# The start of a two-layer kernel, with its first modulation split by chunks and its loads and modulation blocks in another order

## The reference

```
def ada_modulation(cond, w_mod, b_mod):
    m = jax.nn.silu(cond) @ w_mod + b_mod        # (1024) @ (1024, 6144)
    return jnp.split(m, N_MOD, axis=-1)          # shift, scale, gate, shift, scale, gate

# even layer
sh1, sc1, g1, sh2, sc2, g2 = ada_modulation(c, mod_w, mod_b)
csh1, csc1, cg1, csh2, csc2, cg2 = ada_modulation(c_ctx, mod_w, mod_b)
h = modulate(rms_norm(x, norm_mix), sh1, sc1) @ w_in      # w_in: (1024, 2048)
hc = modulate(rms_norm(xc, norm_mix), csh1, csc1) @ w_in
u, q, k, v = jnp.split(h, cuts, axis=-1)
# Fourier mixing of u; neighbourhood attention of q, k, v; x + g1 * (concat @ w_out); dense SwiGLU
```

## Time and profile before

| | us |
|---|---|
| median of 3 runs | 1858.24 (1858.16 to 1859.18) |
| the profiled execution | 1858.6 |
| its span, first to last instruction | 1856.8 |
| TensorE busy | 1787.1 |
| VectorE busy | 1242.8 |
| ScalarE busy | 1008.6 |
| GpSimd busy | 334.8 |

### The profile page before, as it was taken

One profiled execution on the slowest core, in us unless ns is written; L12 is line 12 of the kernel. 1 busy time (PEld: TensorE's weight loads), 2 busy tenths in 40 slices (PEclk: granted clock), 3 DMA queues, 4 the chain that ended last, 5 costly groups with the idle time before them and its releaser, 6 DMA issues.

```text
span 1856.8 us, 24922 instructions
## 1 busy us (share of the span) xinstructions
PE 1787.1 (96%) x8836; PEld 1392.3 (75%) x8836; DVE 1242.8 (67%) x1276; ACT 1008.6 (54%) x1098; POOL 334.8 (18%) x565
## 2 busy tenths in 40 slices
PE   5999999999999999899999999999999999999997
PEld 3667445888888886566788888888888888888886
DVE  3241515242424235745998989989899999998997
ACT  3222834222213121364677777777777777777774
POOL 6886821020201124101100001000000000000000
PEclk8999999999999999999999999999999999999999
DMA  9788612122223151502799999999999999999995
GB/s 371 297 348 302 269 70 91 68 104 100 91 80 125 46 210 57 170 2 91 272 370 383 355 373 364 369 380 355 371 373 361 377 360 366 379 360 373 364 370 205
DMA packets 72503, 481.57 MB, mean 259 GB/s; under 512 B 7984, under 2 KB 11184, under 8 KB 17584
## 3 DMA queue, kind: packets, MB, share of 16 engines
q1 hardware_dynamic: 69872, 472.92, 66.6%
q0 software_dynamic: 1424, 5.51, 0.7%
q10 hardware_dynamic: 1136, 2.21, 0.4%
HBM read 473.29 MB, written 7.32 MB: 259 GB/s over the span
## 4 chain that ended last, share of the span: by engine, by line
PE 90%; DVE 3%; DMA 3%; ACT 2%; issue 1%; SPq 0%; POOL 0%; ACTq 0%; DVEq 0%
PE bank L1090 32%; PE bank L1104 16%; PE bank L807 12%; PE bank L777 4%; PE bank L824 3%; PE bank L836 3%; PE bank L657 3%; PE bank L875 3%; PE bank L590 2%; DMA ring<-in_ev_mod 2%; PE bank L1073 1%; PE bank L745 1%; PE bank L637 1%; PE bank L728 1%; PE bank L1122 1%
## 5 line engine op out<-in xcount | busy, mean ns | idle before, releaser
L1855 DVE TENSOR_TENSOR rest<-ring,WR 128x2048 fp32r<-128x2048 f32 x336 | 765.6, 2306 | 80.6 <-ACT WR L1414 78.8
L1414 ACT ACTIVATE WR<-ring 128x2048 fp32r<-128x2048 f32 x336 | 634.7, 1919 | 68.9 <-DMA ring<-in_experts 66.4
L1090 PE MATMUL bank<-WR,xer 128*128 128x512 f32 x1792 | 579.0, 395 | 2.3 <-DVE B L2032 2.3
L1090 PEld LDWEIGHTS bank<-WR,xer 128*128 128x128 f32 x1792 | 336.4, 188 | 70.0 <-issue 2.5
L1090 PE MATMUL bank<-rest,xer 128*128 128x512 f32 x896 | 349.5, 390 | 0.0
L1104 PE MATMUL bank<-WR,heTr 128*128 128x512 f32 x896 | 279.9, 391 | 0.0
L807 PE MATMUL bank<-hTr,WR 128*128 128x512 f32 x672 | 207.4, 390 | 0.0
L1104 PEld LDWEIGHTS bank<-WR,heTr 128*128 128x128 f32 x896 | 168.2, 188 | 34.5
L1090 PEld LDWEIGHTS bank<-rest,xer 128*128 128x128 f32 x896 | 168.6, 188 | 32.4
L1104 PE MATMUL bank<-rest,heTr 128*128 128x512 f32 x448 | 174.4, 389 | 0.0
L1707 DVE TENSOR_TENSOR rest<-ring,WR 128x2048 fp32r<-128x2048 f32 (+2 forms) x38 | 80.3, 2115 | 123.9 <-ACT WR L1339 123.7
(11 more groups left out here) (354 smaller groups left out, 2143.7 us busy)
## 6 DMA issues: line engine op xcount, KB each, us to landing
ring<-in_experts SPq DMA_DIRECT2D x336, 1024.0 KB, 4.8
ring<-in_ev_mod SPq DMA_DIRECT2D x24, 1024.0 KB, 9.9
ring<-in_od_mod SPq DMA_DIRECT2D x24, 1024.0 KB, 8.3
ring<-in_ffn_up SPq DMA_DIRECT2D x22, 1024.0 KB, 6.9
ring<-in_ffn_down SPq DMA_DIRECT2D x12, 768.0 KB, 5.1
ring<-in_ev_in SPq DMA_DIRECT2D x8, 1024.0 KB, 6.6
ring<-in_ev_out SPq DMA_DIRECT2D x4, 1024.0 KB, 8.3
ring<-in_od_out SPq DMA_DIRECT2D x4, 1024.0 KB, 12.8
```

The source lines that it names most:

```text
L1090: mm = pe.matmul(bank[m % 2][:, :], xer[:, i, 4 * kh + k, :], w[j][:, 512 * k:512 * k + 512], start=(kh == 0 and k == 0 and x == 0), stop= ...
L1414: act.activation(part(0, h), ring[:, h % HALVES, :], ACT.Copy).then_inc(split_hi, 1)
L1855: dve.tensor_tensor(part(1, h), ring[:, h % HALVES, :], part(0, h).bitcast(F32), ALU.subtract).then_inc(split_lo, 1)
```

## The change

**The first modulation is by chunks.** The columns of the first four `ev_mod` slots are regrouped: slot b now holds 256 columns of the shift and 256 of the scale, those of chunks 2b and 2b + 1. Each of blocks 0 to 3 is a group of its own, with its row, its turn and its coefficients (`modulated_front`), and chunks 2b and 2b + 1 are modulated with it. Block 0 stands ahead of the projection, block 1 between the first turn and chunk 0, blocks 2 and 3 ahead of chunks 2 and 3. The 18 products that kept TensorE busy (`keep_busy`) go.

**The loads are reordered.** The first weights of the projection are loaded second, and SP no longer waits for the fourth block's landing before it loads them.

**The blocks are moved.** Blocks 4 to 17 stand in the projection (before: 4 to 16), 18 and 19 in the turns (before: 17), 20, 21 and 22 in the Fourier stage (before: 18), and 23 in step 0 of the attention (before: 19 to 23 in steps 0, 2, 4, 6 and 8). The third group's row and turn go from steps 9 and 10 to steps 1 and 2. The bias tables of heads 5 to 7 are loaded after all modulation blocks.

```
-EARLY = ([("mod", s) for s in range(4)]
-         + [("in", 0), ("mod", 4), ("mod", 5), ("mod", 6), ("in", 1), ("mod", 7), ("mod", 8), ("mod", 9),
...
-UNDER_TURN = {2: 17}
-UNDER_FOUR = {4: 18}
-UNDER_ATTN = {0: 19, 2: 20, 4: 21, 6: 22, 8: 23}
+EARLY = [("mod", 0), ("in", 0), ("mod", 1), ("mod", 2), ("mod", 3),
+         ("in", 1), ("mod", 4), ("mod", 5), ("mod", 6), ("mod", 7),
+         ("in", 2), ("mod", 8), ("mod", 9), ("mod", 10), ("mod", 11),
+         ("in", 3)] + [("mod", s) for s in range(12, 24)]
+EARLY_SLOT = [0, 1, 2, 0, 2, 0, 2, 2, 1, 2, 1, 2, 2, 0, 2, 0, 2, 2, 1, 2, 1, 2, 1, 2, 0, 1, 2, 0]
+UNDER_IN = {(0, 6): 4, (4, 4): 5, (5, 2): 6, (5, 7): 7, (7, 3): 8, (8, 7): 9, (9, 4): 10, (10, 1): 11, (11, 6): 12,
+            (13, 2): 13, (13, 7): 14, (14, 4): 15, (15, 1): 16, (15, 6): 17}
+UNDER_TURN = {3: 18, 7: 19}
+UNDER_FOUR = {2: 20, 4: 21, 7: 22}
+UNDER_ATTN = {0: 23}
-ROW_JOB = 9
+ROW_JOB = 11
-MOD_GROUPS = ((0, 4), (4, 12), (12, 24))
+FRONT = 4
+MOD_GROUPS = ((0, 1), (1, 2), (2, 3), (3, 4), (4, 12), (12, 24))
...
             for i, (what, n) in enumerate(EARLY):
-                if i == S_IN_E[0]:
-                    wait_slot(sp, S_MOD[3])
...
-                if i == S_MOD[22]:
-                    for h in range(5, NA_HEADS):
-                        load_bias(h)
...
+            for h in range(5, NA_HEADS):
+                load_bias(h)
...
             def w_in_even():
+                modulation(1)
                 for c in range(DC):
+                    if c in (2, 3):
+                        modulation(c)
...
+                    if c in (0, 2, 3):
+                        modulation_turn((1, 0, 2, 3)[c])
                 for j in range(4, 16):
                     n, t = divmod(j, 4)
-                    if j == 12:
-                        modulation_turn(1)
+                    if j == 13:
+                        modulation_turn(FRONT)
...
-            for s in range(4):
-                modulation(s)
-                if s == 1:
-                    norm_turn(0)
+            modulation(0)
+            norm_turn(0)
             modulation_turn(0)
-            keep_busy(18)
             w_in_even()
...
+            def modulated_front(b):
+
+                dve.wait_ge(mod_turned, b + 1)
+                o = mod_turn_bank(b)[0]
+                for at, m in ((0, M_SH1 + 2 * b), (4, M_SC1 + 2 * b)):
+                    ins = dve.tensor_tensor(mod[0][:, m:m + 2, :], o[:, at:at + 4].rearrange("p (b s) -> p b s", s=2),
+                                            vec[:, V_MODB + m:V_MODB + m + 2].unsqueeze(2).to_broadcast([P, 2, 2]), ALU.add)
+                step(ins)
+                k = coef[:, 0, 2 * b:2 * b + 2, :]
+                step(dve.tensor_scalar(k, mod[0][:, M_SC1 + 2 * b:M_SC1 + 2 * b + 2, :], 1.0, None, ALU.add))
+                dve.tensor_tensor(k, k, vec[:, V_NORM + 2 * b:V_NORM + 2 * b + 2].unsqueeze(2).to_broadcast([P, 2, 2]),
+                                  ALU.mult).then_inc(coef_front, 1)
+                dve.wait_ge(coef_front, b + 1)
...
             dve.wait_ge(ht_dve, 4)
-            for c in range(1, DC, 2):
+            for b in range(FRONT):
+                c = 2 * b + 1
+                if b:
+                    modulation_row(b)
+                modulated_front(b)
...
-                if c == 1:
+                if b == 0:
                     split_in(0)
...
+                if b == 1:
+                    split_in(1)
```

More of the change, by code:

```diff
@@ L52 @@
 UP_SLOTS, DOWN_SLOTS = FC // 2, 2 * len(FG)
-EARLY = ([("mod", s) for s in range(4)]
-         + [("in", 0), ("mod", 4), ("mod", 5), ("mod", 6), ("in", 1), ("mod", 7), ("mod", 8), ("mod", 9),
-            ("in", 2), ("mod", 10), ("mod", 11), ("mod", 12), ("mod", 13), ("in", 3)]
-         + [("mod", s) for s in range(14, 24)])
-EARLY_SLOT = [0, 1, 2, 0, 1, 2, 0, 2, 0, 2, 2, 1, 2, 1, 1, 0, 1, 0, 1, 2, 1, 2, 1, 2, 1, 2, 0, 1]
-UNDER_IN = {(0, 2): 4, (0, 3): 5, (0, 5): 6, (0, 7): 7, (5, 2): 8, (5, 7): 9, (7, 4): 10, (8, 7): 11, (9, 5): 12,
-            (10, 2): 13, (12, 0): 14, (13, 4): 15, (15, 0): 16}
-UNDER_TURN = {2: 17}
-UNDER_FOUR = {4: 18}
-UNDER_ATTN = {0: 19, 2: 20, 4: 21, 6: 22, 8: 23}
+EARLY = [("mod", 0), ("in", 0), ("mod", 1), ("mod", 2), ("mod", 3),
[8 more added lines that the diff above has]
+UNDER_ATTN = {0: 23}
 ROW_AT = max(UNDER_ATTN) + 1
 IN_BANK = (4, 5, 6, 2)
-ROW_JOB = 9
+ROW_JOB = 11
 S_MOD = [EARLY.index(("mod", s)) for s in range(24)]
 S_IN_E = [EARLY.index(("in", n)) for n in range(4)]
-MOD_GROUPS = ((0, 4), (4, 12), (12, 24))
+FRONT = 4
+MOD_GROUPS = ((0, 1), (1, 2), (2, 3), (3, 4), (4, 12), (12, 24))
 S_OUT_E, S_FFN = 28, 30
@@ L444, in mod_bank @@
         def mod_bank(g):
-            return bank[(0, 3, 7)[g]]
+            return bank[(0, 0, 0, 0, 3, 7)[g]]
         def mod_rows(g):
-            return (mrow[:, 0, :], mrow[:, 1, :], rows[:, 0:512])[g]
+            return rows[:, 0:512] if g == FRONT + 1 else mrow[:, g % 2, :]
         def mod_turn_bank(g):
-            return ((bank[1], 0), (bank[3], 0), (bank[6], 0))[g]
+            return (bank[(1, 1, 1, 1, 3, 6)[g]], 0)
         HALVES2 = (slice(0, HD), slice(HD, 2 * HD))
@@ L1218, in _ @@
             split_in(0)
-            act.wait_ge(coef_ready, 1)
             act.wait_ge(ht_act, 4)
-            for c in range(0, DC, 2):
+            for b in range(FRONT):
+                c = 2 * b
+                act.wait_ge(coef_front, b + 1)
                 for s in range(2):
@@ L1227, in _ @@
                 for cc in (c, c + 1):
-                    act.wait_ge(h0_act if cc == c else h0_dve, cc // 2 + 1)
+                    act.wait_ge(h0_act if cc == c else h0_dve, b + 1)
                     act.activation(h0r[cc], hT[:, cc, :], ACT.Copy).then_inc(h0_hi, 1)
+                if b == 0:
+                    split_in(1)
             act.dma_start(dft, a["dft"]).then_inc(dft_landed, 16)
-            for x in range(1, 4):
+            for x in range(2, 4):
                 split_in(x)
@@ L1603, in _ @@
             normed(0)
+            modulation_row(0)
             for c in range(1, DC, 2):
@@ L1642, in _ @@
                 if j == ROW_JOB:
-                    modulation_row(1)
+                    modulation_row(FRONT)
                 if t in (1, 2) and 1 <= n < 3:
@@ L2358, in strips @@
         return slots(w, [(at, 512) for at in range(0, w.shape[1], 512)])
-    arrays.update(ev_mod=strips(f["ev_mod_w"][0]), ev_in=strips(f["ev_w_in"][0]), od_mod=strips(f["od_mod_w"][0]),
+    w = f["ev_mod_w"][0]
+    first = [w[:, at + 256 * b:at + 256 * b + 256] for b in range(4) for at in (0, D)]
+    arrays.update(ev_mod=strips(np.concatenate(first + [w[:, 2 * D:]], 1)), ev_in=strips(f["ev_w_in"][0]), od_mod=strips(f["od_mod_w"][0]),
                   ev_out=strips(f["ev_w_out"][0]), od_out=strips(f["od_w_out"][0]),
```

18 lines of the change are left out of this document (8 added, 10 removed).

## The result

The changed kernel takes 1861.15 us (median of 20 runs, 1859.19 to 1865.55), the kernel before 1858.65 (20 runs, 1856.89 to 1860.84). The ratio is 1.0016, with a 95% interval of 1.001 to 1.0022: slower by 1.9 to 4.1 us, where 6.2 us faster was forecast. The profiled execution took 1860.71 us, with a span of 1858.8 us.

The account below looks back on a forecast made before the run. TensorE, busy 96% of the span, was taken as the bound, with all gain before 244 us. Fourier stage ending 1.5 us earlier plus attention 4.7 shorter gave 6.2 us off 1858.24: 1852.0 us, range 1849.5 to 1855 (wider: 1846.5 to 1857.5).

Parts of the forecast that it names:

- Part 1: Start of the kernel: first projection matmul at 29.8 us against 45.56, 15.7 us earlier.
- half clock of 2.2 us: Projection's start: TensorE at half clock for some 4 us, costing 2.2 us, bounds 0 and 5.6.
- Part 2: Projection: 124.8 us of work plus 2.2 for the clock and 0.8 of waits, ending at 157.6, 8.7 us earlier.
- the tightest pairs: Projection: ring-slot-sharing blocks 4 and 5, 7 and 8, 8 and 9, with 36 matmuls (8.2 us) between; waits put at 0.8 us.
- Part 3: Turns and Fourier stage: 25.4 us of work with five blocks, plus 1.5 of waits, ending at 184.5 against 186.0.
- 5.2 us a load: Turns and Fourier stage: pace of the modulation loads in a row, landing block 22 at 180.3 us.
- Part 4: Attention: four blocks leave its steps, making it 4.7 us shorter, bounds 1.0 and 7.7.
- Rival 3: Turns and Fourier stage: five loads pace TensorE at 7.1 us each, stage 8 us late, 1861.5 us; chance 0.09.
- bound of 187.2: Fourier stage: its latest end, in us, with loads at 5.8 us each.
- rival 1: Projection and Fourier stage: loads and clock cost nothing, gain 4.5 us more, 1847.5 us; chance 0.17.
- rival 2: Attention: VectorE's and ScalarE's chain replaces the blocks, 1 us won of 5.0, 1855.7 us; chance 0.13.
- rival 4: Front: chunk pipeline at VectorE's pace, three turns wait 2 us each, projection ends 6 us late, 1855 us; chance 0.08.

Follow-up runs that it names:

- e13_spread_both: Changed kernel with blocks 17 to 23 and tables of heads 5 to 7 placed as before, tables of heads 0 to 2 before block 13, GpSimd's stores later; 1848.41 us.
- e11_stores_later: Changed kernel with GpSimd's tables 8 to 12, and so their stores, made behind the bias tables of the attention; 1859.09 us.
- e4_half_loads: Changed kernel with loads of blocks 14 to 22 bringing half their bytes, TensorE multiplying as often; 1851.89 us.
- e12_after_both: Changed kernel with bias tables of heads 0 to 2 loaded before block 13 and GpSimd's stores of tables 8 to 12 behind the bias tables; 1856.77 us.

## Why the prediction was wrong

**Part 1 held.** The first matmul of the projection came at 29.74 us, forecast 29.8. The half clock of 2.2 us did not come; its lower bound, 0, was the value.

**Part 2 was 3 us short.** Its sum without waits and clock, 29.8 + 124.8 = 154.6, agrees with e13_spread_both: 155.52 us with one block less (2.1) and 2.8 us of waits for loads in it, so 154.8 on the same count. Waits were put at 0.8; they were 2.7 before block 14 and 1.7 elsewhere, and 1.5 more of half clock. The step that failed in this part: the tightest pairs were looked for by matmuls between blocks, and block 14's load was not followed through SP's list. It stood behind the 2 MB of block 13 and three tables, all issued in the 3 us before it, and took 14.23 us. The prediction did walk SP's queue past the tables before block 18, not past those before block 14. Its 7.51 us for a lone load was high, too: another load had 0.7 us left to land when that one's second half was issued at 65.94. Two 2 MB loads of the trace before with none ahead of them (second halves issued at 53.58 and 75.93) took 6.86 and 6.98 us, near the 6.8 that the prediction set aside.

**Part 3 is where the forecast broke, in the sentence "block 17 is issued when block 15 is done, at 145.2, and lands near 153".** It was issued at 147.5 and landed at 157.0. 2.3 us of that came with block 15, which ran late behind block 14's wait and half clock. 1.7 came in the queue, 9.5 us from issue to landing where 7.8 was taken: the load of block 16 landed only at 150.81, for the queue had been full since 125 us (399 GB/s to 140 us, 417 from 145 to 186), but for a gap of 5 us with 279 GB/s, when the late block 14 held its slot. A lone load's time was no measure there. Of the 6.3 us by which block 22 landed late (186.56 for 180.3), 4.0 lie there. 1.6 are the pace: five loads in 27.6 us instead of 26.0, because 5.2 us a load stood for 401 GB/s and left out that GpSimd's stores travel in the same stream (4.96 + 0.7, e11_stores_later). 0.7 are the two tables, 2.0 us for 1.3. The stage ended 7.4 us late. The wait that came last in it was the one before block 21, whose load landed at 181.60; block 22's load landed 1.2 us before TensorE came to it at 187.74, while the forecast had looked at block 22 alone. The term for the work, 25.4 us, was nearly right (25.94), and so was the reasoning that TensorE has room: e4_half_loads, in which only the bytes differ, took 1851.9 us, the forecast's time.

**Part 4 held**: 53.75 us, forecast 53.4. **The sum**: 7.4 us up to the Fourier stage's end, 0.3 in the attention and 0.5 in the stages after are 8.2 us in the profiled execution. By the medians the miss is 8.7 us (6.2 forecast and 2.5 the other way) and by the ratio 9.2; the 0.5 to 1.0 us more is the difference between one execution and the medians.

Rival 3 was the case, at 0.09, with its mechanism and with 1861.5 us its time as well. Its numbers were not: it asked for 7.1 us a load from 153 on, and the loads came 5.6 apart from 157 on. It had the Fourier stage 8 us later than before and it was 5.9 later; that the time agrees so well is partly luck, since 0.5 us came from the stages after attention and some 1 us from the difference between one execution and the ratio of the medians. It was priced as if only a slow load could do it, and "loses from over 6.5 us per load" held the start of the stream fixed. A start 4 us late does the same as 0.8 us on each of five loads. And the prediction's own bound of 187.2 for the stage's end had no term for a late start, so the range was too narrow on that side.

The other rivals did not come. Of rival 1 only the clock at the start did. Attention gave 4.4 us, not the 1 of rival 2. No turn or chunk of the front made TensorE wait after its first matmul, so there was no loss as in rival 4.

**What is not settled.** The 0.5 us of the later stages: the same instructions took 1612.4 to 1615.6 us from kernel to kernel in the profiled executions, and no run was made for it. Nor is it shown what a block costs in an odd or a late step of the attention, or what made the 1.2 us in e12_after_both.
